# A two-layer sparse-attention encoder on one core: the k, v and q projections placed ahead of the indexer's dot products

## The reference

```python
proj = h @ w_in
q, k, v, iq, ik, iw, u = jnp.split(proj, SPLIT_POINTS, axis=-1)   # 512, 128, 128, 512, 64, 8, 1024 columns
q = partial_rope(rms_norm(q, q_norm_g), pos, ROPE_DIM)
k = partial_rope(rms_norm(k, k_norm_g), pos, ROPE_DIM)
iq, ik = partial_rope(iq, ...), partial_rope(ik, ...)             # not normed
g = a * jax.nn.sigmoid(b)                                         # u = (a, b), then a causal convolution of width 31
...
dots = jnp.einsum('bqhd,bsd->bqhs', qi, ik_all)                   # the indexer: 8 heads
score = jnp.einsum('bqhs,bqh->bqs', jax.nn.relu(dots), wi)
top_val, top_idx = lax.top_k(score, k_top)                        # 128 or 144 keys of each query
...                                                               # softmax attention over the keys kept
```

## Time and profile before

| | |
|---|---|
| median of three executions | 1631.09 us |
| the profiled execution | 1625.62 us, its span 1623.7 us |
| PE busy | 1297.3 us (80%) |
| DVE busy | 738.0 us (45%) |
| POOL busy | 536.0 us (33%) |
| ACT busy | 336.4 us (21%) |
| DMA | 252.4 MB, 155 GB/s on average |
| mean granted TensorE clock | 0.848 of full |

### The profile page before, as it was taken

One profiled execution on the slowest core, in us unless ns is written; L12 is line 12 of the kernel. 1 busy time (PEld: TensorE's weight loads), 2 busy tenths in 40 slices (PEclk: granted clock), 3 DMA queues, 4 the chain that ended last, 5 costly groups with the idle time before them and its releaser, 6 DMA issues. The chain is left out here.

```text
span 1623.7 us, 13991 instructions
## 1 busy us (share of the span) xinstructions
PE 1297.3 (80%) x5237; PEld 779.0 (48%) x5237; DVE 738.0 (45%) x1370; ACT 336.4 (21%) x756; POOL 536.0 (33%) x325
## 2 busy tenths in 40 slices
PE   7999889855799929999723998897578993999970
PEld 7855525213444427677512554263334442777750
DVE  1108999457723261111134089998773226111113
ACT  2100231104341111111112002312525110111112
POOL 0004999231451100000041049995145110100005
PEclk9999999975589959999866999598557896899995
DMA  9401584460153227999763003011002013699964
GB/s 318 141 8 52 188 304 170 179 288 8 32 164 109 97 92 240 361 352 360 247 209 103 8 26 110 1 59 52 8 1 72 13 45 125 204 365 368 352 221 166
DMA packets 143603, 252.40 MB, mean 155 GB/s; under 512 B 15940, under 2 KB 106412, under 8 KB 138350
## 3 DMA queue, kind: packets, MB, share of 16 engines
q1 hardware_dynamic: 112688, 182.00, 33.4%
q10 hardware_dynamic: 23470, 42.74, 7.7%
q0 software_dynamic: 7376, 26.74, 4.6%
HBM read 225.29 MB, written 30.38 MB: 157 GB/s over the span
## 5 line engine op out<-in xcount | busy, mean ns | idle before, releaser
L392 PE MATMUL ps<-W,arena 128*128 128x256 f32 (+1 forms) x1280 | 349.5, 428 | 7.7 <-ACT arena L1040 2.8
L392 PEld LDWEIGHTS ps<-W,arena 128*128 128x128 f32 x1280 | 241.6, 193 | 85.3 <-issue 47.7
L402 PE MATMUL ps<-C,arena 128*128 128x128 f32 (+4 forms) x847 | 133.0, 308 | 102.3 <-DVE arena L1251 24.8
L392 PE MATMUL ps<-W,hT 128*128 128x512 f32 (+5 forms) x640 | 191.9, 461 | 1.4 <-DVE gt L1111 1.4
L402 PEld LDWEIGHTS ps<-C,arena 128*128 128x128 f32 (+4 forms) x847 | 110.9, 165 | 143.7 <-issue 61.1
L1544 POOL TENSOR_TENSOR arena<-arena 128x512 f32<-128x512 f32 x8 | 89.6, 11198 | 226.9 <-ACT arena L842 226.9
L1180 DVE SCALAR_TENSOR_TENSOR arena<-arena,taps 128x606 f32<-128x606 f32 x180 | 158.9, 952 | 0.2
L392 PEld LDWEIGHTS ps<-W,hT 128*128 128x128 f32 (+1 forms) x640 | 102.4, 181 | 91.3 <-issue 82.4
L1590 POOL DMA_INDIRECT arena<-h_d,idx x32 | 30.3, 948 | 343.5 <-PE ps L402 282.1
L629 PE MATMUL ps<-W,hT 128*128 128x512 f32 (+1 forms) x320 | 142.7, 601 | 1.0 <-issue 1.0
L1574 POOL TENSOR_SCALAR arena<-arena,small 128x128 f32<-128x128 f32 (+4 forms) x80 | 95.4, 1211 | 142.6 <-DVE small L1298 142.6
(11 more groups left out here) (220 smaller groups left out, 1292.0 us busy)
## 6 DMA issues: line engine op xcount, KB each, us to landing
W<-in_w_ada SPq DMA_DIRECT2D x48, 1024.0 KB, 8.5
W<-in_w_gate SPq DMA_DIRECT2D x32, 1024.0 KB, 10.3
W<-in_w_up SPq DMA_DIRECT2D x32, 1024.0 KB, 12.7
W<-in_w_down SPq DMA_DIRECT2D x32, 1024.0 KB, 6.8
y_d<-arena ACTq DMA_DIRECT2D x33, 512.0 KB, 7.1
W<-in_w_in SPq DMA_DIRECT2D x16, 1024.0 KB, 6.0
W<-in_w_out SPq DMA_DIRECT2D x8, 1024.0 KB, 6.9
h_d<-arena ACTq DMA_DIRECT2D x8, 512.0 KB, 2.6
```

Of the source, the lines that this page charges most:

```text
L392: ins = T.matmul(out, l, r, start=n == 0, stop=n == len(pairs) - 1, skip_group_check=True)
L402: count(T.transpose(o, i, ident[0:m, 0:m]), done if n == len(outs_ins) - 1 else None)
```

## The change

The two projections of k, v and q move from behind the 32 dot products to a place ahead of the indexer's transposes, in both layers. PE then waits until all of them have been evacuated (`proja` at 20) before it goes on to `ropei` and `turn_qk`. On ACT the ten evacuations and the two stores of v move ahead of `turned(0, ...)`; they stay behind the wait for `ropei`, the stores of the indexer's k and the issue of the copy into `y_d`. In layer 0 the weights of k, v and q take the use numbers right behind those of the indexer, and ADA1 and ADA2 the ones after, with SP's loop to match; ADA3 to ADA5 keep their numbers. The waits for `proja` at 18 and 19 ahead of ADA3 and ADA4 go. DVE's and POOL's programs are as they were. No computation is added or removed.

```diff
--- before.py
+++ after.py
@@ -242,7 +242,7 @@
                 dve.sem_inc(go[name], 1)
 
         MIX0 = 8
-        U_ADA1, U_ADA2, U_KV, U_Q = MIX0 + 8, MIX0 + 16, MIX0 + 24, MIX0 + 26
+        U_KV, U_Q, U_ADA1, U_ADA2 = MIX0 + 8, MIX0 + 10, MIX0 + 12, MIX0 + 20
         U_ADA3, U_ADA4, U_ADA5, U_OUT0 = MIX0 + 28, MIX0 + 36, MIX0 + 44, MIX0 + 52
         EXP0 = U_OUT0 + 4
         MIX1 = EXP0 + 3 * NE
@@ -336,10 +336,9 @@
                 load(i, wada[0, :, :, 256 * i:256 * i + 256])
             for l in range(DEPTH):
                 for c in range(8):
-                    if l == 0 and c == 4:
+                    if l == 0 and c == 6:
                         ada(U_ADA1, 0)
                         ada(U_ADA2, 1)
-                    if l == 0 and c == 6:
                         ada(U_ADA3, 2)
                         ada(U_ADA4, 3)
                         ada(U_ADA5, 4)
@@ -495,6 +494,10 @@
                         turn([(ps[6][0:30, c * P:(c + 1) * P], gT[:, c, 512:542]) for c in range(4)], L["cst"])
                         turn([(ps[7][0:30, c * P:(c + 1) * P], gT[:, c, 606:636]) for c in range(4)], L["cst"])
 
+                project(4, 256, 10, (0, 1, 2), L["proja"], L["proj"])
+                project(5, 512, 15, (0, 1, 2), L["proja"], L["proj"])
+                pe.wait_ge(L["proja"], 20)
+
                 def turn_qk(src, past, job):
 
                     for i in range(5):
@@ -525,12 +528,8 @@
                 if l == 0:
                     pe.wait_ge(s_adae, 3)
 
-                project(4, 256, 10, (0, 1, 2), L["proja"], L["proj"])
-                project(5, 512, 15, (0, 1, 2), L["proja"], L["proj"])
                 if l == 0:
-                    pe.wait_ge(L["proja"], 18)
                     ada(ps[2], U_ADA3, range(KC), 2)
-                    pe.wait_ge(L["proja"], 19)
                     ada(ps[0], U_ADA4, range(KC), 3)
 
                 pe.wait_ge(L["rel"], 32)
@@ -884,6 +883,13 @@
 
                 if l == 0:
                     act.dma_start(y_d[XROW:XROW + XJ * P, :], A["w_out"][0]).then_inc(s_fill, 16)
+                for job in range(10, 15):
+                    out_of(job)
+                act.wait_ge(L["proja"], 15)
+                store("new_v_prompt", tiles, vrow[:, 0:4, :])
+                store("new_v_sample", row, vrow[0:DEC, 4, :])
+                for job in range(15, 20):
+                    out_of(job)
                 turned(0, kT[0])
 
                 for n, (t, h) in enumerate((t, h) for t in SCORED for h in range(8)):
@@ -899,15 +905,8 @@
                     if l == 0 and n == 25:
                         keep_mod(0)
 
-                for job in range(10, 15):
-                    out_of(job)
-                act.wait_ge(L["proja"], 15)
-                store("new_v_prompt", tiles, vrow[:, 0:4, :])
-                store("new_v_sample", row, vrow[0:DEC, 4, :])
                 if l == 0:
                     keep_mod(1)
-                for job in range(15, 20):
-                    out_of(job)
                 act.wait_ge(L["proja"], 20)
                 act.wait_ge(L["outst"], 96)
                 for t in range(NT):
```

## The result

| | kernel before | changed kernel |
|---|---|---|
| median, four executions each on one chip | 1632.65 us (1630.67 to 1635.23) | 1669.95 us (1668.88 to 1672.00) |
| ratio, 95% interval | | 1.0229 (1.0208 to 1.025) |
| profiled execution, its span | 1625.62 us, 1623.7 us | 1668.95 us, 1667.0 us |
| mean granted TensorE clock | 0.848 | 0.840 |

The change costs 37.3 us, 2.3%. The lines of the changed kernel stand one lower than before: L391 is the projections' line (L392 before), L1232 the sums of squares (L1233), L430 the slices of `w_ada` (L431), L1196 and L1199 the scores, L1554 to L1560 POOL's convolution.

What follows compares the result with a forecast made beforehand. Waits between engines were taken to bound the stages, PE's 53 us of projections lying beside DVE's 48 us of selection. Layers' 6.6 + 38.7 = 45.3 us on the median 1631.09 gave 1676.4 us; range 1655 to 1688.

Steps and rivals of the forecast that it cites:

- the likeliest case: Both layers: projections delay DVE's scores and the selection loses its cover; 1676.4 us, alone 1671 to 1682, chance 0.80.
- (a): PE ahead of the dot products: 53.3 us of projections run without a stall, so the transposes start 48.3 us later.
- The rival in which they would not get into the hole: PE's projections held back until 1005.5 by ACT or late weights: 5.6 us more per layer, 1687.6 us, chance 0.05.
- (b): DVE ahead of its first score: stands still for 45.7 us in layer 1; layer 0's first score moves by 45.6 us.
- (f): Load order, earlier stores of v and PE's low clock after the selection: taken as nothing, clock bounded at 0 to 2 us per layer.
- (c): POOL in DVE's wait: a tap every 3.24 us, so it ends before the scores and gives back 2 us per layer.
- POOL faster alone: POOL in DVE's wait: about 2.3 us per tap, giving 12.4 us back per layer, 1655.6 us, chance 0.09.
- the one that pays the wait back: POOL finishes its taps within DVE's wait, so scores and taps cost 25.8 us; 1632.5 us, no slower, chance 0.02.
- (d): Layer 1's selection runs alone on DVE, no longer beside the projections; the sums of squares start 38.7 us later.
- (e): Layer 0: the waits for ADA3 and ADA4, 37.0 us, go, so the sums start only 6.6 us later.
- the sum's last one: Whole kernel: the 45.3 us difference, worked out on the profiled execution, added to the median of three, 1631.09, giving 1676.4 us.

Runs made afterwards that it cites:

- shortened kernels: The 18 selection rounds for tile 4 left out in both layers: in the kernel before 1632.78 us, in the changed kernel 1626.46 us.
- the two other traces with the old order there: Kernel before with tile 4's 18 selection rounds left out (1632.78 us), and kernel before with the new order in layer 1 only (1666.28 us).

## Why the prediction was right, and where it was off

Slower was right, and so was the likeliest case: 1676.4 us were forecast and 1669.95 us measured, inside the range, while the 1671 to 1682 of that case alone begins 1 us too high. The working was made for a difference of 45.3 us; the stages gave 41.6 us and the timing 37.3 us.

**(a) The projections on PE: right.** They run for 52.25 us without a gap in both layers. POOL's first tap to the transposes took 1005.48 - 998.75 = 6.73 us before and takes 1060.16 - 1006.27 = 53.89 us now: 47.2 us later, forecast 48.3. The 1.1 us is that PE's projections took 52.25 us and not the 53.3 of the chain of waits, and this is the clock: in layer 1 of the kernel before they took 53.32 us, with a granted clock of 0.79 in the first 4.7 us (1061.23 to 1065.95), behind the dot products; now it is 1.00 throughout. In layer 0 they had 1.00 and 52.35 us before as well. The rival in which they would not get into the hole falls: no row shows a wait of PE inside them.

**(b) DVE's wait: right in kind, 2.9 us too large in each layer.** 42.8 us instead of 45.7. Beside the 1.1 us above, this is a term that the sum did not have: what the clock gives back at the indexer's transposes. These 25 take 2.85 us in both layers at a granted clock of 1.00, where PE comes to them 0.67 us after the projections; before, behind a hole of 5.6 us, they took 4.34 us and 4.36 us at 0.64 and 0.65. That is 1.5 us of the 2.9, and 0.3 us are left. The "0 to 2 us" of (f) was a bound on what a low clock could cost at the later transposes, behind the selection.

**(c) POOL's pace: right, and its term too large.** With DVE idle POOL starts a tap every (1062.09 - 1026.66) / 11 = 3.22 us, against the 3.24 us taken from the selection. With this the rival "POOL faster alone" falls, and with it the one that pays the wait back: the 0.84 us pass is a form of its own, and is recorded with 0.84 us again now. The Trainium skill (GPSIMD Engine Reference, Specifications) names two kinds of VectorE instruction that contend with GpSimd: those with two SBUF inputs and those in a 2-port mode. The prediction counted the selection to neither, and POOL's pace agrees: a tap every 3.24 us under the selection and every 3.22 us with DVE idle. The 0.76 and 1.40 us of a tap in the prediction are not the same measure: 0.76 us is the time from one start to the next, and the recorded mean of a held-off tap, which compares with 1.40 us, is 0.834 us (54 taps, layer 0 of the changed kernel). The factor is 1.7. The scores gave back 0.7 us in layer 1 (48.72 against 49.42) and 1.4 us with the selection in layer 0, where I had taken 2: POOL ends at 1114.7, 0.3 us ahead of the last score, and not 4.2 us ahead. POOL's own end was right (108.4 us after its first tap, forecast 108.05); what takes its lead away is that the scores start 2.9 us sooner than forecast.

**(d) The selection alone: right.** 48.29 us on DVE, 6.86 us on PE, no wait ahead of the sums. The account of layer 1 closes: 42.8 (wait) - 0.7 (scores) - 5.0 (the squares) + 0.1 = 37.2 us, forecast 38.7. The shortened kernels show the cause itself: the 18 rounds are worth nothing before and some 43 us after.

**(e) Layer 0: right, a little less.** The slices are done at 332.8, forecast at 333.5. No wait ahead of the bias additions. 42.8 - 1.4 - 37.0 = 4.4 us, forecast 6.6; against the two other traces with the old order there 2.5 and 3.0 us.

**(f) Edits at nothing: right.** Load order, stores of v and the clock in the selection (0.57 in layer 1) cost nothing behind the sums: the stretch to the end is 1.5 us shorter, not longer, and the 25 transposes of q and k in layer 1 took 4.26 us, against 5.04 before.

**The step that missed by most is the sum's last one.** The difference was worked out against one profiled execution and added to the median, as if the stretch outside the terms were the same in every execution. Of the 8.0 us between 45.3 and 37.3, 3.7 are the terms above (41.6 us in the stages). The other stretches add 1.7 us in the profiled pair, which makes 43.3. But the profiled execution of before lies 7.0 us under the median of its group (1625.62 against 1632.65), and that of the changed kernel 1.0 us under its own: 43.3 - 6.0 = 37.3 us. (The forecast of 1676.4 us misses by 6.4 and not 8.0 us, because it was added to a median of 1631.09, and a fourth execution made that 1632.65.) 25 executions of the kernel before in one job lie between 1626.84 and 1636.62 us, median 1632.43, all above the profiled one.

Two things vary in the traces with the old order in layer 0. The stage of layer 0 ends with the last slice of weights (155.68, 157.12 and 157.64 us); the changed kernel, bound by DVE there, has no use for an early arrival. And attention and experts of layer 0 last 656.65 us in the trace of before and 661.0 us in the other two. That is not the weights: PE waits for them for 1.3 to 1.5 us in all three. It is busy for 524 us instead of 517, with the same 2147 matmuls, at a mean granted clock of 0.83 instead of 0.85. The 25 executions point the same way: the four fastest (under 1628 us) show a mean clock of 0.849 to 0.853, the four slowest (over 1635.5 us) 0.843 to 0.847. Why the clock differs from one execution to the next, and how the 6.0 us divide between the two, no run shows.

## What to carry to other kernels

Before work of one engine is moved to fill a hole, look at what lies beside it in its old place: here 5.6 us of hole were filled with 53 us that had covered 48 us of another engine. Move no more than the hole and the next engine's own slack can take (k and v, 17.6 us, gained 0.6%, and with DVE's taps put into the rest of the wait 1.4%). And if the last thing to end is work that nobody needs yet, such as weight slices for later, move that back rather than the rest forward: it was worth nearly half of the 2.5% here (from 0.9864 to 0.9748), once the small store that it held up was issued first.

## What the runs showed of the hardware

**DVE's two-operand instructions against POOL.** The scores and taps of a layer take 29.65 us with POOL at rest and 48.72 us beside its convolution. By form, in the scores of layer 1 (count, busy, mean ns, idle before), the changed kernel:

```profile
L1179 DVE SCALAR_TENSOR_TENSOR arena<-arena,taps 128x606 f32<-128x606 f32 x11 | 14.9, 1359 | 0.0
L1199 DVE SCALAR_TENSOR_TENSOR arena<-arena,iw 128x512 f32<-128x512 f32 x7 | 9.4, 1342 | 0.4
```

and with POOL left out:

```profile
L1179 DVE SCALAR_TENSOR_TENSOR arena<-arena,taps 128x606 f32<-128x606 f32 x11 | 9.2, 841 | 0.0
L1199 DVE SCALAR_TENSOR_TENSOR arena<-arena,iw 128x512 f32<-128x512 f32 x7 | 5.2, 750 | 0.4
```

Factors of 1.6 and 1.8 on DVE. While POOL is held off (see below) the tap has a mean of 0.834 us, about the same as with POOL at rest; started back to back, one follows the other every 0.76 us. Instructions with one tensor as input are of both kinds. The eight-largest and match-replace rounds show nothing of POOL: the selection takes 48.24 us beside it and 48.29 us without. But the first score of a tile, a `tensor_scalar` with one tensor as input (L1196, 128x512), took 0.98 us in either layer of the changed kernel and 0.47 us in either layer with POOL at rest.

**The other way round, POOL can be held off altogether.** In layer 0 of the changed kernel, POOL in order of time; the last one lies under an unbroken row of DVE's taps, which ends at 185.88 (46 of such a row):

```profile
128.71 1.27 POOL L1543 TENSOR_TENSOR arena<-arena 128x512 f32<-128x512 f32 x1 [15.76 <-ACT arena L841]
146.02 41.00 POOL L1543 TENSOR_TENSOR arena<-arena 128x512 f32<-128x512 f32 x1 [15.76 <-ACT arena L841]
```

The same form of instruction is recorded with 1.27 and 41.00 us. The long one ends at 187.02, 1.1 us after the row of taps, which is about what it takes otherwise; layer 1 has the same (40.99 us). A POOL instruction that otherwise takes 1.3 us was over only when the row of such DVE work beside it was.

**Small stores amid a stream of weights.** 256 KB landed in 12.5 and 13.9 us, and 32 KB, issued 0.4 us behind it on the same queue, in 13.9 and 14.9 us, in stretches full of 1 MB loads, in which 363 and 422 GB/s were moved in all; in the kernel before stores of both forms took 2.3 and 2.1 us. Whether the small one would have been quicker by itself is not shown.
